# A two-layer hybrid decoder trunk with retrieved experts on one core: routing and gates head by head, the other heads beside a pair's own gathers

## The chip, the cores and the metric

One core of one Trainium2 chip runs the whole program in one launch. The time is device microseconds, from the start to the end of the execution. Engines are named as the profile names them: PE (TensorE), DVE (VectorE), ACT (ScalarE), POOL (GpSimd), SP (SyncE, which here only issues transfers).

## What is computed

512 tokens of width 1024 in float32 pass two layers. In each, a normalised input is projected and goes through three mixers (a Mamba-2 scan, stick-breaking attention, native sparse attention), whose outputs are projected and added to x. Then comes the expert layer:

```python
def block(xb):                                   # 128 tokens
    q = (xb @ w_q).reshape(Tb, PEER_HEADS, 2, half)            # 8 heads, two halves of 128
    s = jnp.einsum('thpd,pkd->thpk', q, sub_keys)              # 128 keys each
    sv, si = lax.top_k(s, PEER_TOPK)                           # 16
    cand = sv[:, :, 0, :, None] + sv[:, :, 1, None, :]
    cv, ci = lax.top_k(cand.reshape(Tb, PEER_HEADS, PEER_TOPK * PEER_TOPK), PEER_TOPK)
    i1 = jnp.take_along_axis(si[:, :, 0, :], ci // PEER_TOPK, axis=-1)
    i2 = jnp.take_along_axis(si[:, :, 1, :], ci % PEER_TOPK, axis=-1)
    eidx = i1 * N_KEYS + i2                                    # one of 16384 experts
    g = jax.nn.softmax(cv, axis=-1)
    u = u_tab[eidx]; v = v_tab[eidx]
    a = jax.nn.gelu(jnp.einsum('thkd,td->thk', u, xb))
    return jnp.einsum('thk,thkd->td', (g * a), v)
```

So each token reads 8 x 16 = 128 rows of 4 KB from each of two tables, its own rows.

## The kernel before

**Pairs, steps, slots.** The four blocks of 128 tokens go in pairs. A step is one pair of one layer; there are four (STEPS = 4). A step has a trunk (norm, mixers, output projection), a routing (queries, top 16, indices, gates), and 256 slots of gathers (PER_STEP): slot s reads one expert row for each of 128 tokens. POOL issues for each slot one indirect transfer of 512 KB from the u table (L1455) and, LAG = 20 slots later, one of 512 KB from the v table (L1468). Row buffers are rings of six (U_RING, V_RING): POOL may issue the u rows of slot s when the dot product of slot s - 6 is done.

**Who uses the rows.** DVE multiplies each u row by the normalised token and sums it (a dot, L1393). After 16 slots ACT takes the gelu and DVE multiplies by the gates (L1400). A v row is added to the output either by PE, as a product with a diagonal matrix of the weights (L741, two matmuls of 512 columns into `acc`, the diagonal made by ACT, L1021), or by DVE as one multiply-add (L1410). `of_vector` says which: before, DVE takes 1 of 2 while a trunk runs beside, 1 of 16 otherwise, and 1 of 4 in the last step. At a block's end `acc` is added to x (L1415).

**Order.** Each engine runs in the order of its program. The trunk and the routing are cut in phases (PHASES: n1a, ..., u0 to u24, cz, t0, ..., o0, ..., then the routing r0 to r22, each r from 4 on in three pieces r, rb, rc, and g0 to g2). SLOT_OF gives each phase a slot, and each engine, after its part of slot s, runs the phases due by s. Before, step 0's trunk and whole routing run first, with nothing gathered; then in the gathers of step n the trunk of step n + 1 stands in slots 22 to 146 and its routing in 146 to 253. The last step's gathers have nothing beside them.

**Routing.** Phase r k computes on PE the queries of half-head k (k = 0 to 15) and the scores of half-head k - 2; ACT copies both out of PSUM, the scores only when DVE is done with the half-head two before (`top`). DVE takes the top 16 of half-head k - 4 for both blocks, of the 256 sums of head (k - 6) // 2 for one block, and decodes the choice of k - 7 into table rows. After r22, g0 turns all eight heads' choices into indices at once (L1356, L1357: signal `idx`), ACT exponentiates all gates, g2 normalises them. POOL waits for `idx` once for each step; DVE waits for `gate` at each block's start (L1386).

Of the kernel before, what the change touches and what calls it, by code (L numbers as in the profile page):

```python
# [15 lines left out]
EXPERTS = KEYS * KEYS  # L17
# [134 lines left out]
def phases():  # L152
# [28 lines left out]
    tail += [("g0", 0, .4), ("g1", 0, 0), ("g2", 0, 1.2)]  # L181
# [17 lines left out]
SLOT_OF = slots()  # L199

# [4 lines left out]
           g_sub=1, g_exp=1, gate=1, idx=1, h2=2)  # L205


def trunk(nc, x_dram, const_dram, param_dram, w_dram, u_dram, v_dram, out_dram):
# [4 lines left out]
    with ctx:  # L213
# [163 lines left out]
        class Phases:  # L377


            def __init__(self, tracks):  # L380
                self.tracks = [[t, next(t)] for t in tracks]
                self.done = 0

            def upto(self, last):
                while self.done <= last:
                    for track in self.tracks:
                        while track[1] == PHASES[self.done][0]:
                            track[1] = next(track[0], None)
                    self.done += 1
                if last == len(PHASES) - 1:  # L390
                    assert all(at is None for _, at in self.tracks), self.tracks
# [22 lines left out]
        def phase_after(n, slot):  # L414

            return int((SLOT_OF <= slot - (n - 1) * PER_STEP).sum()) - 1

# [306 lines left out]
        def tensor_program(pe):  # L724
            run = Phases(tensor_tracks(pe, 0))
            run.upto(len(PHASES) - 1)
            for s in range(GATHERS + LAG):
                n = s // PER_STEP + 1
                if s % PER_STEP == 0 and n < STEPS:
                    run = Phases(tensor_tracks(pe, n))  # L730
# [13 lines left out]
                if n < STEPS:  # L744
                    run.upto(phase_after(n, s))


        def scalar_tracks(act, n, chain):
# [219 lines left out]
            def out_():  # L968
# [11 lines left out]
                for k in range(1, 2 * PEER_H + 3):  # L980
# [7 lines left out]
                    if k >= 3:  # L988
# [11 lines left out]
        def scalar_program(act):  # L1000
            chain = InOrder(act, "scalar_chain")
            run = Phases(scalar_tracks(act, 0, chain))
            run.upto(len(PHASES) - 1)
            for s in range(GATHERS + LAG):
                n = s // PER_STEP + 1
                if s % PER_STEP == 0 and n < STEPS:
                    run = Phases(scalar_tracks(act, n, chain))
# [14 lines left out]
                if n < STEPS:  # L1022
                    run.upto(phase_after(n, s))


        def vector_tracks(dve, n, chain):
# [295 lines left out]
            def route():  # L1322
# [46 lines left out]
        def vector_program(dve):  # L1369
# [3 lines left out]
            for s in range(GATHERS + LAG):  # L1373
# [42 lines left out]
                if n < STEPS:  # L1416
                    run.upto(phase_after(n, s))
# [125 lines left out]
```

## Time and profile before

| what | us |
|---|---|
| three runs: median (lowest, highest) | 3396.27 (3394.38, 3422.13) |
| the profiled execution, its own time | 3410.22 |
| its span on the profile page | 3408.4 |
| granted TensorE clock, mean | 0.924 |
| DVE, PE, POOL, ACT busy, share of the span | 69%, 78%, 66%, 23% |
| indirect transfers | 2048, 1073.9 MB |
| read from HBM over the span | 1183 MB, 348 GB/s |

The page cuts the span in 40 slices of 85.2 us; a digit is the busy share of a slice in tenths. The profiled execution's own time stands 14 us over the median, so a difference is worked out inside the profile and then taken from the median. A window of a view names its start and end from the span's start, and the x in it counts instructions; where a window is cut at POOL's issues of L1455, that count is its number of slots.

### The profile page before, as it was taken

To read this page: it belongs to the slowest core of one execution; us is meant where nothing else is said; L and a number is where in the kernel's file an instruction comes from. 1 tells how busy PE (TensorE), PEld (TensorE's weight loads), DVE (VectorE), ACT (ScalarE), POOL (GpSimd) and SP (SyncE) were. 2 spreads that over 40 slices of the span, in tenths; PEclk is the share of its full clock that TensorE was granted. 3 is DMA by queue.
4 is the path that set the end of the run, shared out by engine and by line. 5 is a ranking of instruction groups with operands and counts; after the bars stand their busy time and mean duration, and the time that the engine had idled before them with its cause. 6 is when DMAs were issued, how large, how long until landed. Compare 5 with 4: busy or idle time off the path is not lost.

```text
span 3408.4 us, 30404 instructions
## 1 busy us (share of the span) xinstructions
PE 2653.3 (78%) x9120; PEld 1550.1 (45%) x9120; DVE 2352.5 (69%) x5335; ACT 769.2 (23%) x1848; POOL 2260.1 (66%) x2059
## 2 busy tenths in 40 slices
PE   8888079898987689778987679988987666556657
PEld 7677057556543256446543246656543222112212
DVE  2327975877689576877699666877689755666564
ACT  2531023442211123332111122442211111111111
POOL 0000276777777776777777776777677777777776
PEclk9879589989999999878999999989999989998899
DMA  5112399999999999999999999999999999999999
GB/s 184 59 50 92 115 385 412 366 322 392 410 362 358 388 410 412 390 331 381 410 381 379 358 383 411 378 322 367 410 394 355 364 401 409 409 409 408 410 409 349
DMA packets 311313, 1187.53 MB, mean 348 GB/s; under 512 B 34544, under 2 KB 34544, under 8 KB 298352
## 3 DMA queue, kind: packets, MB, share of 16 engines
q0 software_dynamic: 294912, 1073.87, 81.8%
q1 hardware_dynamic: 16240, 111.72, 8.4%
q8 instruction: 75, 1.23, 0.1%
q14 instruction: 86, 0.70, 0.1%
HBM read 1183.36 MB, written 2.10 MB: 348 GB/s over the span
## 4 chain that ended last, share of the span: by engine, by line
POOL 30%; PE 26%; DMA 22%; issue 10%; DVE 4%; ACT 1%; ACTq 0%; DVEq 0%; POOLq 0%
DMA v_rows<-expert_v,idx 22%; POOL u_rows L1455 16%; POOL v_rows L1468 15%; PE acc L741 14%; PE bank L457 4%; PE bank L448 4%; DVE arena L1030 1%; PE bank L620 1%; PE bank L439 1%; DVE arena L1288 0%; PE bank L540 0%; DVE arena L1280 0%; DVE arena L1292 0%; DVE X L1410 0%; DVE arena L1318 0%
## 5 line engine op out<-in xcount | busy, mean ns | idle before, releaser
L741 PE MATMUL acc<-v_rows,diag 128*128 128x512 f32 x2988 | 1533.6, 647 | 647.4 <-DMA v_rows<-expert_v,idx 575.6
L1393 DVE CUSTOM_DVE_ANT_0 u_rows<-u_rows,h 128x1024 f32<-128x1024 f32 x1024 | 1247.9, 1224 | 650.5 <-DMA u_rows<-expert_u,idx 646.1
L1455 POOL DMA_INDIRECT u_rows<-expert_u,idx x1024 | 1122.4, 1096 | 685.4 <-DVE idx L1357 348.9
L1468 POOL DMA_INDIRECT v_rows<-expert_v,idx x1024 | 1133.9, 1107 | 404.3 <-issue 249.3
L741 PEld LDWEIGHTS acc<-v_rows,diag 128*128 128x128 f32 x2988 | 560.1, 203 | 1453.1 <-issue 1177.3
L1021 ACT ACTIVATE diag<-consts,wgt 128x128 f32<-128x128 f32 x747 | 286.2, 397 | 1097.8 <-PE acc L741 882.2
L448 PE MATMUL bank<-HT,w_ring 128*128 128x256 f32 x1792 | 405.1, 381 | 2.1 <-DVE HT L1030 2.1
L1410 DVE SCALAR_TENSOR_TENSOR X<-v_rows,wgt,X 128x1024 f32<-128x1024 f32 x277 | 355.7, 1284 | 56.4 <-DMA v_rows<-expert_v,idx 50.7
L448 PEld LDWEIGHTS bank<-HT,w_ring 128*128 128x128 f32 x1792 | 341.3, 191 | 81.3 <-issue 38.7
L457 PE MATMUL bank<-w_ring,HT 128*128 128x256 f32 (+1 forms) x1280 | 274.7, 372 | 0.0
L457 PEld LDWEIGHTS bank<-w_ring,HT 128*128 128x128 f32 x1280 | 236.7, 191 | 50.0 <-issue 21.4
L753 ACT ACTIVATE arena<-bank 128x256 f32<-128x256 f32 (+4 forms) x304 | 112.5, 382 | 505.4 <-PE bank L448 223.6
L1013 ACT ACTIVATE gel<-dots 128x16 f32<-128x16 f32 x64 | 13.8, 216 | 418.4 <-DVE dots L1393 418.3
L1030 DVE TENSOR_TENSOR arena<-arena 128x256 f32<-128x256 f32 (+3 forms) x238 | 102.4, 433 | 5.2 <-ACT arena L753 3.5
L1393 DVE DVE_READ_ACCUMULATOR2_ANT dots<- 128x1 f32 x1024 | 83.1, 81 | 0.0
L1280 DVE MAX8 arena<-arena 128x8 f32<-128x128 f32 (+1 forms) x192 | 52.8, 327 | 15.6 <-ACT arena L753 13.4
L620 PE MATMUL bank<-arena,w_ring 64*64 64x32 f32 x512 | 47.4, 267 | 20.1 <-issue 20.1
L670 PE MATMUL bank<-nkT,arena 64*128 64x128 f32 (+3 forms) x128 | 58.8, 545 | 3.5 <-ACT arena L949 3.5
L439 PE MATMUL bank<-dg,X 128*128 128x128 f32 x256 | 38.2, 318 | 28.9 <-ACT dg L753 28.9
L1288 DVE MATCH_REPLACE8 arena<-arena 128x128 f32<-128x128 f32 (+1 forms) x192 | 59.5, 318 | 0.0
L1030 DVE TENSOR_TENSOR HT<-bank,params 128x512 f32<-128x512 f32 x48 | 31.5, 685 | 40.3 <-PE bank L439 40.2
L1030 DVE TENSOR_TENSOR arena<-arena,consts 128x256 f32<-128x256 f32 (+3 forms) x168 | 58.6, 387 | 0.7
(185 smaller groups left out, 1860.1 us busy)
## 6 DMA issues: line engine op xcount, KB each, us to landing
w_ring<-weights SPq DMA_DIRECT2D x100, 1024.0 KB, 8.0
u_rows<-expert_u,idx POOLq DMA_INDIRECT x1024, 7.9
v_rows<-expert_v,idx POOLq DMA_INDIRECT x1024, 7.9
X<-in_x SPq DMA_DIRECT2D x2, 1024.0 KB, 6.5
out<-X SPq DMA_DIRECT2D x4, 512.0 KB, 6.5
n2w_wide<-parameters SPq DMA_DIRECT2D x2, 512.0 KB, 8.0
params<-parameters SPq DMA_DIRECT2D x2, 412.0 KB, 7.8
consts<-constants SPq DMA_DIRECT2D x1, 749.5 KB, 6.3
```

Of the source, the lines that this page charges most:

```text
L439: last = T.matmul(out[:, blk[i]], src[:, k * P:(k + 1) * P], dg[:, at_d + b], start=True, stop=True)
L448: last = T.matmul(out[:, 0:PAIR], cols(i)[:, k, m % 2 * P:(m % 2 + 1) * P], HT[:, k, :], start=(k == 0), stop=(k == KT - 1))
L457: last = T.matmul(out[:, 0:width], HT[:, k, blk[b]], cols(i)[:, k, 0:width], start=(k == 0), stop=(k == KT - 1))
L620: last = T.matmul(out[0:64, 0:CMP_PAD], weights[lo:lo + 64, j, :], cmp_z[lo:lo + 64, j, :], start=(j == 0), stop=(j == CMP_LEN - 1))
L741: last = T.matmul(acc[:, at_h], diag[:, i % DIAG_RING], v_rows[:, t % V_RING, at_h], start=(at_t == 0), stop=(t == max(q for q in range(t ...
L753: return S.activation(dst, src, ACT.Copy, **k)
L1021: made(S.activation(diag[:, i % DIAG_RING], ident, ACT.Copy, scale=wgt[:, b % 2, at_t:at_t + 1]), "diag")
L1030: return V.tensor_tensor(out, in0, in1, op)
L1393: made(V.tensor_tensor_reduce(out=rows_u, in0=rows_u, in1=h2[:], scale=1.0, scalar=0.0, op0=ALU.mult, op1=ALU.add, accum_out=dots[:, b % 2 ...
L1410: made(V.scalar_tensor_tensor(Xb, v_rows[:, t % V_RING, :], wgt[:, b % 2, at_t:at_t + 1], Xb, ALU.mult, ALU.add), "v_used_vector")
L1455: pool.indirect_dma_start(out=u_rows[:, s % U_RING, :], out_offset=None, in_=u_dram, in_offset=bass.IndirectOffsetOnAxis(ap=idx[:, (n - 1) ...
L1468: pool.indirect_dma_start(out=v_rows[:, t % V_RING, :], out_offset=None, in_=v_dram, in_offset=bass.IndirectOffsetOnAxis(ap=idx[:, t // PE ...
```

## The change

Routing and gates are made head by head. Indices of a head and block are formed as soon as they are decoded (`chosen`), a head's gates two phases later (`gated`), and POOL waits for the indices of the first block at every head. The phases before r8, which give head 0 of the first block, stay ahead of the pair's gathers; the rest, r8 to r22 and g2, stand beside the pair's own gathers in slots 1 to 86. The next trunk and its r0 to r7 follow in slots 90 to 254. DVE takes 1 of 2 v rows wherever the row's slot plus 20 is 90 or more (1 of 4 in the last step), 1 of 16 below that. The number of v rows that DVE adds goes from 71, 71, 71, 64 in the four steps to 97, 97, 97, 51.

```diff
@@
-TRUNK_AT, ROUTE_AT, DONE_AT = LAG + 2, 146, PER_STEP - 3
+
+ROUTED_AT, TRUNK_AT, FIRST_AT = 86, 90, PER_STEP - 2
 
 def of_vector(t):
     step, slot = divmod(t, PER_STEP)
-    if step == STEPS - 1:
-        return t % 4 == 3
-    return t % 2 == 1 if TRUNK_AT <= slot + LAG < ROUTE_AT else t % 16 == 15
+    if slot + LAG < TRUNK_AT:
+        return t % 16 == 15
+    return t % 4 == 3 if step == STEPS - 1 else t % 2 == 1
@@
-    tail += [("g0", 0, .4), ("g1", 0, 0), ("g2", 0, 1.2)]
+    tail += [("g2", 0, .5)]
@@
+FIRST = ORDER["r8"]
+
 def slots():
-    work = np.array([max(cost) + .5 for _, *cost in PHASES])
-    at, out = ORDER["r0"], []
-    for part, lo, hi in ((work[:at], TRUNK_AT, ROUTE_AT), (work[at:], ROUTE_AT, DONE_AT)):
-        out += list(lo + (np.cumsum(part) - part) / part.sum() * (hi - lo))
-    return np.array(out)
+    work = np.array([max(cost) + .5 for _, *cost in PHASES[:FIRST]] + [cost[1] + .5 for _, *cost in PHASES[FIRST:]])
+    spread = lambda part, lo, hi: lo + (np.cumsum(part) - part) / part.sum() * (hi - lo)
+    before_, beside = spread(work[:FIRST], TRUNK_AT - PER_STEP, FIRST_AT - PER_STEP), spread(work[FIRST:], 1, ROUTED_AT)
+    out = [n * PER_STEP + np.concatenate([before_ if n else np.full(FIRST, -1), beside]) for n in range(STEPS)]
+    return np.concatenate(out)
@@
+assert all(SLOT_OF[ORDER[f"r{7 + 2 * h}c"]] <= 16 * h - 5 for h in range(1, PEER_H))
@@ PER: how often each signal is given in a step
-           g_sub=1, g_exp=1, gate=1, idx=1, h2=2)
+           g_sub=8, g_exp=8, gate=8, idx=16, h2=2)
@@
-        def phase_after(n, slot):
-            return int((SLOT_OF <= slot - (n - 1) * PER_STEP).sum()) - 1
+        def phases_after(slot):
+            return int((SLOT_OF <= slot).sum())
@@ all four engine programs, as the tensor engine's
-            run = Phases(tensor_tracks(pe, 0))
-            run.upto(len(PHASES) - 1)
+            run = Phases(lambda n: tensor_tracks(pe, n))
+            run.upto(phases_after(-1))
             for s in range(GATHERS + LAG):
-                n = s // PER_STEP + 1
-                if s % PER_STEP == 0 and n < STEPS:
-                    run = Phases(tensor_tracks(pe, n))
...
-                if n < STEPS:
-                    run.upto(phase_after(n, s))
+                run.upto(phases_after(s))
@@ scalar_tracks, out_
-                yield "g1"
-                act.wait_ge(sig("g_sub"), nth(n, "g_sub", 1))
-                made(S.activation(g[:, n % 2], g[:, n % 2], ACT.Exp), "g_exp")
+                    if k >= 8 and k % 2 == 0:
+                        h = (k - 8) // 2
+                        at_h = g[:, n % 2].rearrange("p (b h k) -> p b h k", b=2, h=PEER_H)[:, :, h]
+                        act.wait_ge(sig("g_sub"), nth(n, "g_sub", h + 1))
+                        made(S.activation(at_h, at_h, ACT.Exp), "g_exp")
@@ vector_tracks, route
-                yield "g0"
-                g3 = g[:, n % 2].rearrange("p (b h k) -> p b h k", b=2, h=PEER_H)
+                        if b:
+                            made(tt(gates(h), cv[:, :, h], cv[:, :, h, 0:1].to_broadcast([P, 2, TOPK]), ALU.subtract), "g_sub")
+                    if 0 <= c - 1 < 2 * PEER_H:
+                        chosen(*divmod(c - 1, 2))
+                    if k >= 9 and k % 2:
+                        gated((k - 9) // 2)
+                yield "g2"
+                gated(PEER_H - 1)
+
+            def chosen(h, b):
                 chain.upto(chain.n)
-                made(tt(g3, cv, cv[:, :, :, 0:1].to_broadcast([P, 2, PEER_H, TOPK]), ALU.subtract), "g_sub")
-                chain(V.scalar_tensor_tensor(picked[:, 1], picked[:, 0], float(KEYS), picked[:, 1], ALU.mult, ALU.add))
-                made(V.tensor_scalar(idx[:, n % 2], picked[:, 1].rearrange("p b s -> p (b s)"), float(l * EXPERTS), None, ALU.add), "idx")
-                yield "g2"
-                dve.wait_ge(sig("g_exp"), nth(n, "g_exp", 1))
-                gsum = sm["gsum"][:].rearrange("p (b h) -> p b h", b=2)
-                chain(V.tensor_reduce(gsum, g3, AX.X, ALU.add))
-                chain(V.reciprocal(sm["grec"][:], sm["gsum"][:]))
-                made(tt(g3, g3, over(sm["grec"][:].rearrange("p (b h) -> p b h", b=2), TOPK)), "gate")
+                at_h = slice(h * TOPK, (h + 1) * TOPK)
+                chain(V.scalar_tensor_tensor(picked[:, 1, b, at_h], picked[:, 0, b, at_h], float(KEYS), picked[:, 1, b, at_h],
+                                             ALU.mult, ALU.add))
+                made(V.tensor_scalar(idx[:, n % 2, b * SLOTS + h * TOPK:b * SLOTS + (h + 1) * TOPK], picked[:, 1, b, at_h],
+                                     float(l * EXPERTS), None, ALU.add), "idx")
+
+            def gated(h):
+                dve.wait_ge(sig("g_exp"), nth(n, "g_exp", h + 1))
+                gsum, grec = (sm[name][:].rearrange("p (b h) -> p b h", b=2)[:, :, h] for name in ("gsum", "grec"))
+                chain(V.tensor_reduce(gsum, gates(h), AX.X, ALU.add))
+                chain(V.reciprocal(grec, gsum))
+                made(tt(gates(h), gates(h), over(grec, TOPK)), "gate")
@@ vector_program
                     if at_s == 0:
-                        m = n - 1
-                        dve.wait_ge(sig("rs5"), nth(m, "rs5", 1))
-                        dve.wait_ge(sig("gate"), nth(m, "gate", 1))
-                        dve.wait_ge(sig("n2w_in"), 16 * (m // PAIRS + 1))
+                        dve.wait_ge(sig("rs5"), nth(n, "rs5", 1))
+                        dve.wait_ge(sig("n2w_in"), 16 * (n // PAIRS + 1))
@@
                     dve.wait_ge(sig("gelu"), head + 1)
+                    dve.wait_ge(sig("gate"), nth(b // 2, "gate", head % PEER_H + 1 if b % 2 == 0 else PEER_H))
@@ pool_program
-                    if s % PER_STEP == 0:
-                        pool.wait_ge(sig("idx"), n)
+                    head = s % PER_STEP // TOPK
+                    if s % TOPK == 0 and head <= PEER_H:
+                        pool.wait_ge(sig("idx"), nth(n, "idx", 2 * head + 1 if head < PEER_H else 2 * PEER_H))
...
-                    run.upto(phase_after(n, s - POOL_LAG) if s % PER_STEP < PER_STEP - 1 else len(PHASES) - 1)
+                run.upto(phases_after(s - POOL_LAG))
```

Three places show what moves. On DVE at the start of the first gathers, after the first routing, before the change (g and idx are the gates and the indices, ISA is a dot and the read of its sum, h the normalised token):

```order
L1030 TENSOR_TENSOR g<-arena 128x256
L1356 SCALAR_TENSOR_TENSOR arena<-arena 128x256
L1357 TENSOR_SCALAR idx<-arena 128x256
L1361 TENSOR_REDUCE sm_gsum<-g 128x16
L1362 RECIPROCAL sm_grec<-sm_gsum 128x16
L1030 TENSOR_TENSOR g<-g,sm_grec 128x256
L1386 SCALAR_TENSOR_TENSOR h<-X,sm_rs,n2w_wide 128x1024
L1393 ISA u_rows,dots<-u_rows,h 128x1024
```

The same place after the change, which comes when only r0 to r7 have run:

```order
L1036 TENSOR_TENSOR g<-arena 128x2x16
L1375 SCALAR_TENSOR_TENSOR arena<-arena 128x16
L1377 TENSOR_SCALAR idx<-arena 128x16
L1405 SCALAR_TENSOR_TENSOR h<-X,sm_rs,n2w_wide 128x1024
L1412 ISA u_rows,dots<-u_rows,h 128x1024
L1412 ISA dots 128x1
L1412 ISA u_rows,dots<-u_rows,h 128x1024
L1412 ISA dots 128x1
L1036 TENSOR_TENSOR arena<-arena 128x256
L1286 MAX arena<-arena 128x8 x3
```

The indices cover 16 columns and not 256, and r8's top-16 work (the last two rows) now stands behind the first two dots.

On DVE after the change, across the boundary between steps 0 and 1 (the first rows are the end of r7's piece rc; L1430 is a v row added by DVE):

```order
L1036 TENSOR_TENSOR g<-arena 128x2x16
L1375 SCALAR_TENSOR_TENSOR arena<-arena 128x16
L1377 TENSOR_SCALAR idx<-arena 128x16
L1412 ISA u_rows,dots<-u_rows,h 128x1024
L1412 ISA dots 128x1
L1412 ISA u_rows,dots<-u_rows,h 128x1024
L1412 ISA dots 128x1
L1430 SCALAR_TENSOR_TENSOR X<-v_rows,wgt,X 128x1024
L1405 SCALAR_TENSOR_TENSOR h<-X,sm_rs,n2w_wide 128x1024
```

Two dots (slots 254 and 255) stand between the indices and the next step's normalised token (`h`); before, the indices came one slot earlier, ahead of the dots of 253 to 255.

On POOL at the first gathers after the change, with what each row waits for:

```order
L1473 DMA u_rows<-expert_u,idx 128x1024 [waits idx,tail]
L1473 DMA u_rows<-expert_u,idx 128x1024 x5
L1473 DMA u_rows<-expert_u,idx 128x1024 [waits u_used] x10
L1473 DMA u_rows<-expert_u,idx 128x1024 [waits u_used,idx]
L1473 DMA u_rows<-expert_u,idx 128x1024 [waits u_used] x4
L1486 DMA v_rows<-expert_v,idx 128x1024
```

A second wait for `idx` stands at slot 16 and again at every 16th slot up to 128: nine in a step, where there was one.

## Rows read from the trace of the kernel before

**Rows 1.** The page: busy shares, then tenths busy in 40 slices, and GB/s.

```profile
PE 2653.3 (78%) x9120; PEld 1550.1 (45%) x9120; DVE 2352.5 (69%) x5335; ACT 769.2 (23%) x1848; POOL 2260.1 (66%) x2059
...
POOL 0000276777777776777777776777677777777776
...
GB/s 184 59 50 92 115 385 412 366 322 392 410 362 358 388 410 412 390 331 381 410 381 379 358 383 411 378 322 367 410 394 355 364 401 409 409 409 408 410 409 349
```

**Rows 2.** The u transfers (L1455) alone, by step; the last step in three.

```profile
core 0: us, POOL busy (x), PEclk, DMA share, GB/s
397.85:1148.22 750.37, 293.88 (x256) 0.94 0.98 374
1148.22:1924.55 776.33, 291.27 (x256) 0.93 0.99 385
1924.55:2701.85 777.30, 285.97 (x256) 0.95 0.99 376
2701.85:2927.00 225.15, 83.11 (x86) 0.92 1.02 402
2927.00:3363.00 436.00, 167.72 (x170) 0.94 1.03 409
```

**Rows 3.** All engines by stretch: routing alone, first gathers, step 1's trunk, its routing, two 16-slot stretches.

```profile
core 0: us, PE busy (x) PEld busy (x) DVE busy (x) ACT busy (x) POOL busy (x), PEclk, DMA share, GB/s
275.00:296.00 21.00, 21.00 (x109) 18.75 (x108) 17.89 (x99) 3.44 (x11) 0.00 (x0) 1.00 0.35 121
296.00:397.00 101.00, 35.11 (x158) 29.07 (x156) 99.01 (x466) 6.78 (x20) 0.00 (x0) 0.70 0.13 48
397.85:425.00 27.15, 0.00 (x0) 0.00 (x0) 20.02 (x33) 0.22 (x1) 21.31 (x20) 0.50 0.91 325
...
1209.70:1592.80 383.10, 324.24 (x1297) 214.00 (x1296) 287.20 (x475) 118.12 (x277) 285.26 (x251) 0.90 0.99 382
1592.80:1924.55 331.75, 270.95 (x794) 141.95 (x793) 268.75 (x814) 60.23 (x158) 256.46 (x220) 0.97 1.00 385
1828.40:1877.10 48.70, 36.70 (x76) 14.13 (x74) 48.15 (x169) 7.42 (x21) 38.95 (x33) 0.91 0.98 370
3117.50:3158.40 40.90, 28.29 (x48) 11.03 (x48) 24.82 (x38) 4.81 (x13) 31.18 (x32) 0.83 1.03 409
```

**Rows 4.** POOL's waits in step 1's trunk stretch, 1209.70 to 1592.80: total, times, longest.

```profile
POOL u_rows L1455 <- issue: 36.5, 120, 0.3
POOL v_rows L1468 <- issue: 32.3, 106, 0.3
POOL v_rows L1468 <- PE acc L741: 23.5, 18, 4.3
POOL u_rows L1455 <- DVE dots L1393: 5.5, 4, 2.4
```

**Rows 5.** The page's groups: dots, their reads, DVE's v rows.

```profile
L1393 DVE CUSTOM_DVE_ANT_0 u_rows<-u_rows,h 128x1024 f32<-128x1024 f32 x1024 | 1247.9, 1224 | 650.5 <-DMA u_rows<-expert_u,idx 646.1
...
L1410 DVE SCALAR_TENSOR_TENSOR X<-v_rows,wgt,X 128x1024 f32<-128x1024 f32 x277 | 355.7, 1284 | 56.4 <-DMA v_rows<-expert_v,idx 50.7
...
L1393 DVE DVE_READ_ACCUMULATOR2_ANT dots<- 128x1 f32 x1024 | 83.1, 81 | 0.0
```

**Rows 6.** DVE in order of time: the first rows of r7 and of r8; then idx.

```profile
288.53 0.43 DVE L1030 TENSOR_TENSOR arena<-arena 128x256 f32<-128x256 f32 x1
...
295.86 0.43 DVE L1030 TENSOR_TENSOR arena<-arena 128x256 f32<-128x256 f32 x1
...
396.69 0.29 DVE L1357 TENSOR_SCALAR idx<-arena 128x256 uint32<-128x256 f32 x1
```

**Rows 7.** POOL in order of time: the first gather.

```profile
397.90 1.14 POOL L1455 DMA_INDIRECT u_rows<-expert_u,idx  x1 [348.88 <-DVE idx L1357]
```

**Rows 8.** DVE in order of time, end of step 0's gathers: idx.

```profile
1145.27 0.29 DVE L1357 TENSOR_SCALAR idx<-arena 128x256 uint32<-128x256 f32 x1
```

**Rows 9.** POOL in order of time: step 1's first u transfer.

```profile
1148.27 0.93 POOL L1455 DMA_INDIRECT u_rows<-expert_u,idx  x1 [0.30 <-issue]
```

More of the change, by code:

```diff
@@ L377, in trunk, with __init__, upto @@
         class Phases:
[L380 to L385, printed above, removed]
+            def __init__(self, tracks_of):
+                self.tracks_of, self.done = tracks_of, 0
+            def upto(self, count):
+                while self.done < count:
+                    n, i = divmod(self.done, len(PHASES))
+                    if i == 0:
+                        self.tracks = [[t, next(t)] for t in self.tracks_of(n)]
                     for track in self.tracks:
-                        while track[1] == PHASES[self.done][0]:
+                        while track[1] == PHASES[i][0]:
                             track[1] = next(track[0], None)
                     self.done += 1
-                if last == len(PHASES) - 1:
-                    assert all(at is None for _, at in self.tracks), self.tracks
+                    if i == len(PHASES) - 1:
+                        assert all(at is None for _, at in self.tracks), self.tracks
         def over(scalars, n):
@@ L979, in out_ @@
                     diagonal("5", b, 0)
-                for k in range(1, 2 * PEER_H + 3):
+                for k in range(1, 2 * PEER_H + 7):
                     yield f"r{k}"
@@ L1001, in scalar_program @@
             chain = InOrder(act, "scalar_chain")
-            run = Phases(scalar_tracks(act, 0, chain))
-            run.upto(len(PHASES) - 1)
+            run = Phases(lambda n: scalar_tracks(act, n, chain))
+            run.upto(phases_after(-1))
             for s in range(GATHERS + LAG):
-                n = s // PER_STEP + 1
-                if s % PER_STEP == 0 and n < STEPS:
-                    run = Phases(scalar_tracks(act, n, chain))
                 if s % TOPK == 0 and 0 < s <= GATHERS:
@@ L1021, in scalar_program @@
                     made(S.activation(diag[:, i % DIAG_RING], ident, ACT.Copy, scale=wgt[:, b % 2, at_t:at_t + 1]), "diag")
-                if n < STEPS:
-                    run.upto(phase_after(n, s))
+                run.upto(phases_after(s))
         def vector_tracks(dve, n, chain):
@@ L1370, in vector_program @@
             chain = InOrder(dve, "vector_chain")
-            run = Phases(vector_tracks(dve, 0, chain))
-            run.upto(len(PHASES) - 1)
+            run = Phases(lambda n: vector_tracks(dve, n, chain))
+            run.upto(phases_after(-1))
             for s in range(GATHERS + LAG):
-                n = s // PER_STEP + 1
-                if s % PER_STEP == 0 and n < STEPS:
-                    run = Phases(vector_tracks(dve, n, chain))
+                n = s // PER_STEP
                 if s < GATHERS:
@@ L1415, in vector_program @@
                     made(V.tensor_tensor(Xb, acc[:], Xb, ALU.add), "x_done")
-                if n < STEPS:
-                    run.upto(phase_after(n, s))
+                run.upto(phases_after(s))
         def pool_tracks(pool, n, chain):
@@ L1442, in pool_program @@
             chain = InOrder(pool, "pool_chain")
-            run = Phases(pool_tracks(pool, 0, chain))
-            run.upto(len(PHASES) - 1)
+            run = Phases(lambda n: pool_tracks(pool, n, chain))
+            run.upto(phases_after(-1))
             for s in range(GATHERS + LAG):
-                n = s // PER_STEP + 1
-                if s % PER_STEP == 0 and n < STEPS:
-                    run = Phases(pool_tracks(pool, n, chain))
+                n = s // PER_STEP
                 if s < GATHERS:
-                    if s % PER_STEP == 0:
-                        pool.wait_ge(sig("idx"), n)
+                    head = s % PER_STEP // TOPK
+                    if s % TOPK == 0 and head <= PEER_H:
+                        pool.wait_ge(sig("idx"), nth(n, "idx", 2 * head + 1 if head < PEER_H else 2 * PEER_H))
                     if s >= U_RING:
```

8 lines of the change are left out of this document (5 added, 3 removed).

## Prediction

> **What bounds the kernel now.** I began with the page. No engine is busy all through, and for the first four and a half of 40 slices POOL does nothing while from then on the bytes come at 320 to 412 GB/s [rows 1]. So the program has two parts: a start without gathers, and a stretch in which something paces them. The time line of POOL dates the border: its first transfer starts at 397.90, 348.88 us late, released by `idx` [rows 7].
>
> The second part is 3010.5 us, and the windows of the u transfers cut it by steps [rows 2]: 750.4, 776.3, 777.3, then 225.2 for the first 86 slots of the last step, 436.0 for the other 170, and 3408.4 - 3363.0 = 45.4 behind them. A slot costs 2.93, 3.03, 3.04, 2.62 and 2.56 us. I read what paces it from three rows [rows 3]:
> - With nothing beside (3117.50 to 3158.40, 16 slots, 2.56 a slot) POOL is busy 31.18 us in 32 transfers, 0.97 each, and rests 0.30 before each: 2 x (0.97 + 0.30) = 2.55. POOL's own issuing is the pace; DVE is busy 61%.
> - Beside the densest routing (1828.40 to 1877.10, 16 slots, 3.04 a slot) the transfers take 38.95 / 33 = 1.18 and the rest is the same: 2 x 1.48 = 2.96. DVE is busy 99%. POOL waits for nobody, each issue is longer.
> - Beside the trunk (1209.70 to 1592.80, 124 slots, 3.09 a slot) a transfer takes 285.3 / 251 = 1.14. POOL idled for PE 23.5 us in 18 times, for DVE 5.5 in 4 [rows 4]; less the 0.3 that stands before any transfer that is 22 us. Without them the pace is (383.1 - 22) / 124 = 2.91.
>
> So outside the start the kernel is at POOL's issue rate, 2.56 us a slot when DVE is loosely used and about 2.9 to 3.0 when it is dense, plus waits where PE is late.
>
> **The start.** Before, r8 to r22 stand between the end of r7 and the indices. r8's first row starts at 295.86, the indices at 396.69 [rows 6], POOL 1.21 behind them [rows 7]. After, r7 ends with three small rows (gates' subtraction, two for the indices), 0.6 us by the gaps of the rows around them, so indices are made at 296.5 and the first transfer starts at 297.7. That is **-100.2 us**. Nothing hides it and nothing is uncertain in it but tenths; all that can be lost is what the moved work costs further on: 99.0 us of DVE and 35.1 of PE [rows 3].
>
> **DVE's load of a slot.** A dot is 1224 + 81 ns, so 1.30; a v row on DVE 1284 ns [rows 5]: 0.64 a slot where it takes 1 of 2, 0.08 at 1 of 16. A full routing phase is 295.86 - 288.53 = 7.3 us [rows 6]. The trace has no per-head gates and indices. Eight small rows a head replace six wide ones; between 0.1 (all pipelined) and 0.3 us each (the indices' row took 0.29) gives 0.8 to 2.4 us a head; less 0.3 for the removed share I take 1.3, 0.65 a phase, 10 us in a step. With 5.65 slots between phases (85 slots, 15 phases) the routing is (7.3 + 0.65) / 5.65 = 1.41 a slot.
>
> **Slots 0 to 20 of steps 1 to 3.** The v rows of the previous step's end are still half DVE's: 1.30 + 0.64 + 1.41 + 0.1 for normalising and closing a block (two rows of 1024 columns, like those of [rows 5], in 20 slots) = 3.45. That is over POOL's 2.96, so here DVE would be the pace. POOL runs two to five dots ahead and the ring allows six, so up to 10 us of it could be absorbed (low end 2.96 a slot); I charge it in full: 69 us.
> **Slots 0 to 20 of step 0.** No v rows. DVE needs 2.8 a slot; POOL issues slot 20 when dot 14 is done: 5 us to the first landing + 14 x 2.8 = 44 us, against 28 before (20 transfers in 27.15 us, as DVE keeps up with the dots alone) [rows 3].
> **Slots 20 to 86.** DVE 1.30 + 0.08 + 1.41 = 2.8, a little under the dense row's 3.0. Pace 2.95 (bounds: 2.75, half way between the loose and the dense row; 3.10, the dense row's 3.04 with the added small rows on top): 66 x 2.95 = 195.
> **Slots 86 to 90.** Nothing beside: 10 us.
> **The trunk, n1a to n2a, slots 90 to 233.** The same work on 143 slots instead of 124, so the parts on PE are 13% less dense. No-wait pace 2.90 as now, 415 us; PE's waits, 22 us now, I halve to 12 (bounds 0 and 22): 427. PE's load falls on the whole (DVE takes 26 v rows more in a step, each two matmuls fewer for PE).
> **r0 to r7, slots 233 to 256.** DVE's part (275 to 296) is 17.9 us [rows 3], plus 1.3, in the last 17 slots: 1.13 + 1.94 = 3.07 and lumps of up to 3 us. I charge 3.15 x 23 = 73.
> **The boundary.** Before, the indices were made at 1145.27 [rows 8] and POOL needed them at 1148.27 [rows 9], 3 us to spare. After, they follow dot 253, one slot later, and 3.1 us of r7's last piece: at about 1150.5, and later when DVE is behind, as it is there. Queued behind POOL's wait are the v transfers of slots 236 on. I charge 5 us at each of three boundaries (bounds 0, if POOL is held up anyway, and 12, with DVE three rows behind).
>
> The nine waits for `idx` in a step cost nothing by the order: head 1 is due after slot 10 and asked for at 16, the others have more. The cover is six dots, 17 us; without it each would cost its lateness. The new wait for `gate` is met seven slots ahead.
>
> **The sum**, in the profile's own time:
>
> | step | before | after | difference |
> |---|---|---|---|
> | start | 397.9 | 297.7 | -100.2 |
> | 0 | 750.4 | 44 + 195 + 10 + 427 + 73 = 749 | -1 |
> | 1 | 776.3 | 5 + 69 + 195 + 10 + 427 + 73 = 779 | +3 |
> | 2 | 777.3 | 779 | +2 |
> | 3, to slot 86 | 225.2 | 5 + 69 + 195 = 269 | +44 |
> | rest | 481.4 | the same | 0 |
>
> Together -52: 3410.2 becomes 3358. The median stands 14 lower, so the forecast is **3344 us**.
>
> **A page's rule against the rows.** In the stretch with nothing beside, DVE is 61% busy with dots and v rows alone, and POOL's transfers take 0.97; beside routing they take 1.18 with the same number of dots [rows 3].
> The Trainium skill, page "SBUF — State Buffer", section "Who interferes with whom", says that a DVE instruction with two SBUF inputs contends with a GpSimd instruction that reads SBUF, and one with at most one does not (outside the two-port modes). Dots and v rows have two such inputs; top-16 rows have one. By it alone slots 20 to 86 would stay near 2.6 a slot, 23 us a step less than I charge. The row on routing disagrees, so the sum goes by the row; no run here separates the forms of instruction.
>
> **Rivals.**
> - *Forecast (0.50).* As summed; its own range 3318 to 3370.
> - *The cover is cheaper (0.17).* Routing spread over 85 slots leaves DVE at 2.8 a slot, and issues lengthen only where DVE is really full. Then slots 20 to 86 go at 2.75 (-13 in each of four steps) and the overload of slots 0 to 20 is absorbed by the ring (-10 in three): 3344 - 82 = 3262 at the most; half of that is likelier, 3303. For it: POOL at 1.14 beside the trunk, where DVE is 75% busy; against it: beside the routing of step 1 DVE is busy 81% and a transfer takes 256.5 / 220 = 1.17 already.
> - *DVE becomes the bound (0.22).* From slot 239 of a step to 20 of the next, 37 slots, DVE's need is over POOL's pace. If its in-order waits (for ACT's copies, for v rows that are late) add 0.15 us a slot there and in slots 20 to 86, that is 3 x 37 + 4 x 66 = 375 slots x 0.15 = 56 us. The gain is gone: 3400. For it: 99% busy in the dense stretch; against: POOL did not wait for DVE even there.
> - *Indices come late, head by head (0.11).* POOL's wait at a head holds the v transfers behind it too, and PE and DVE behind those. There are 28 new heads; from 52 / 28 = 1.9 us of lateness each the gain is gone, and at 5 us each, two slots, the kernel takes 3344 + 140 = 3484; at 3.5 us it takes 3442. For it: DVE will run late in slots 0 to 20, where head 1 has only six slots of cover; against: heads 2 to 7 gain 4.7 slots of cover each.
>
> **How the numbers follow.** About 1%, 34 us, is what a measurement of this kernel can tell from no change: faster is under 3362, slower over 3430. The forecast lies under 3362 in nine tenths of its weight: 0.45 + 0.17 = 0.62 faster; the rest of the forecast, the third case and a little of the last are within 1%: 0.28; slower 0.10, nearly all from late indices. The range must leave out no more than 0.2. Below it goes to the second case, 3303, rounded to 3300 (both cheap ends in full, 3262, are the tail that is left out); above it takes in the third case, 3400.
>
> **What would show it.** POOL's first u transfer at 297.7. In the windows by step, 749, 779, 779, and 269 for the first 86 slots of the last, then again 2.56 a slot. POOL's mean transfer near 1.17 in slots 20 to 86 of the last step, where it was 0.98. DVE over 95% busy in slots 240 to 276. POOL waiting for `idx` at three boundaries for some 5 us and at the heads not at all; its waits for PE in the trunk stretch halved. The prediction is wrong if POOL waits for dots or indices by tens of microseconds, or if a step's 256 slots take under 765 or over 795.

## The result, and the profile after

| | before | after |
|---|---|---|
| median of 20 runs each, us | 3410.88 | 3389.13 |
| lowest, highest | 3393.79, 3434.49 | 3373.11, 3405.5 |
| the profiled execution | 3410.22 | 3384.28 |
| its span | 3408.4 | 3382.5 |

The ratio is 0.9931, 95% interval [0.9912, 0.9950]: 22 us, or 0.7%, where 52 us, 1.5%, had been forecast. That is faster, but less than half as much as I said, and by my own bound of 1% it is no change. The profiled executions, in whose time the sum was made, differ by 25.9 us. (The median of three runs shown ahead of the prediction, 3396.27, was 15 us low. The sum does not hang on it, the 3344 does: from the 20 runs it would have been 3359.)

The page of after, the lines that answer to [rows 1]:

```profile
PE 2623.9 (78%) x8860; PEld 1549.2 (46%) x8860; DVE 2455.5 (73%) x5632; ACT 810.0 (24%) x1860; POOL 2313.6 (68%) x2059
...
POOL 0002777767776787767775777767777678777776
...
GB/s 183 62 41 193 360 368 375 412 410 354 347 399 355 365 340 389 411 411 368 348 390 365 387 369 359 388 411 343 356 370 411 351 358 337 363 408 408 409 409 360
```

POOL starts a good slice earlier, and the stretch at 408 to 410 GB/s at the end is shorter, with 337 to 363 ahead of it. The u transfers of after by step, as in [rows 2]:

```profile
core 0: us, POOL busy (x), PEclk, DMA share, GB/s
297.75:1061.73 763.98, 289.97 (x256) 0.91 0.98 373
1061.73:1849.00 787.27, 287.85 (x256) 0.90 0.98 376
1849.00:2639.00 790.00, 286.13 (x256) 0.91 0.98 374
2639.00:2899.05 260.05, 104.54 (x86) 0.91 0.95 350
```

The first transfer starts at 297.78, where 297.7 was forecast. A window here runs up to the next step's first transfer, so the boundary's 5 us belong to the step before it: forecast were 754, 779 and 779, and 264 for the last step's first 86 slots. The steps take 764, 787 and 790 us, the 86 slots 260.

All engines of after, by stretches (slots 20 to 86, 90 to 233 and 233 to 256 of step 0; then slots 0 to 20 and 20 to 86 of the last step):

```profile
core 0: us, PE busy (x) PEld busy (x) DVE busy (x) ACT busy (x) POOL busy (x), PEclk, DMA share, GB/s
340.10:533.45 193.35, 136.61 (x328) 58.52 (x328) 174.21 (x570) 41.83 (x99) 152.19 (x132) 0.95 0.98 366
544.00:977.50 433.50, 381.04 (x1565) 249.74 (x1564) 325.62 (x526) 142.41 (x309) 330.88 (x287) 0.93 0.99 380
977.50:1061.73 84.23, 67.15 (x254) 46.30 (x252) 67.26 (x171) 14.99 (x36) 53.03 (x46) 0.91 0.97 390
...
2639.00:2698.40 59.40, 34.93 (x96) 19.72 (x96) 53.74 (x148) 8.27 (x21) 46.49 (x40) 0.80 0.94 356
2698.40:2899.05 200.65, 144.43 (x352) 65.20 (x352) 174.51 (x564) 41.66 (x98) 159.73 (x132) 0.94 0.95 348
```

The third row is the one that stands out: 23 slots in 84.2 us, 3.66 a slot. What POOL did there, in order of time:

```profile
1045.71 1.14 POOL L1473 DMA_INDIRECT u_rows<-expert_u,idx  x1 [0.30 <-issue]
1047.16 0.95 POOL L1486 DMA_INDIRECT v_rows<-expert_v,idx  x1 [0.30 <-issue]
1061.75 1.67 POOL L1473 DMA_INDIRECT u_rows<-expert_u,idx  x1 [13.65 <-DVE idx L1377]
```

and DVE, up to the indices that POOL waits for (the first two rows are the dot of slot 253 and a v row, the rest the end of r7):

```profile
1056.38 1.22 DVE L1412 CUSTOM_DVE_ANT_0 u_rows<-u_rows,h 128x1024 f32<-128x1024 f32 x1
...
1057.52 1.28 DVE L1430 SCALAR_TENSOR_TENSOR X<-v_rows,wgt,X 128x1024 f32<-128x1024 f32 x1
...
1059.65 0.72 DVE L1324 TENSOR_REDUCE arena<-arena 128x16 f32<-128x256 f32 x2
...
1061.31 0.17 DVE L1377 TENSOR_SCALAR idx<-arena 128x16 uint32<-128x16 f32 x1
```

POOL issued slot 255 at 1045.71, as early as the ring of six allows: dot 249 was done, dot 250 in hand. Ahead of the indices DVE still had the rest of that dot, dots 251 to 253, two v rows and the last pieces of r6 and r7, and it did them with hardly a gap, busy 15.19 of 15.60 us (columns as above, from POOL's issue to the row of `idx`):

```profile
1045.71:1061.31 15.60, 9.08 (x30) 4.92 (x28) 15.19 (x58) 0.96 (x3) 2.09 (x2) 0.84 0.77 312
```

POOL stood still 13.65 us; at the two later boundaries 14.90 and 13.65. Before, the indices had been 3 us early.

### The profile page after: what moved, and what is told of

The parts are those of the page before. It is cut to its first block, busy times and chain, and to the rows that moved or that the text cites. A ratio compares the mean times of both kernels' runs of the same rounds, so it can differ in the third digit from the quotient of the medians.

```text
span 3382.5 us, 30188 instructions
## 1 busy us (share of the span) xinstructions
PE 2623.9 (78%) x8860; PEld 1549.2 (46%) x8860; DVE 2455.5 (73%) x5632; ACT 810.0 (24%) x1860; POOL 2313.6 (68%) x2059
## 4 chain that ended last, share of the span: by engine, by line
POOL 33%; PE 22%; DMA 20%; issue 11%; DVE 6%; ACT 1%; DVEq 0%; ACTq 0%; POOLq 0%
DMA v_rows<-expert_v,idx 18%; POOL v_rows L1486 17%; POOL u_rows L1473 16%; PE acc L750 13%; PE bank L469 3%; PE bank L460 3%; DMA u_rows<-expert_u,idx 2%; DVE u_rows L1412 2%; PE bank L632 1%; DVE X L1430 1%; PE bank L451 1%; DVE arena L1036 1%; DVE arena L1286 0%; DVE arena L1294 0%; DVE arena L1298 0%
## 5 line engine op out<-in xcount | busy, mean ns | idle before, releaser
L750 PE MATMUL acc<-v_rows,diag 128*128 128x512 f32 x2728 | 1489.1, 683 | 672.6 <-DMA v_rows<-expert_v,idx 598.3
L1473 POOL DMA_INDIRECT u_rows<-expert_u,idx x1024 | 1134.1, 1108 | 625.0 <-issue 303.2
L1486 POOL DMA_INDIRECT v_rows<-expert_v,idx x1024 | 1177.0, 1149 | 385.6 <-issue 259.4
L750 PEld LDWEIGHTS acc<-v_rows,diag 128*128 128x128 f32 x2728 | 534.4, 212 | 1417.0 <-issue 1181.4
L1430 DVE SCALAR_TENSOR_TENSOR X<-v_rows,wgt,X 128x1024 f32<-128x1024 f32 x342 | 439.7, 1286 | 73.6 <-DMA v_rows<-expert_v,idx 67.1
L1028 ACT ACTIVATE diag<-consts,wgt 128x128 f32<-128x128 f32 x682 | 256.1, 395 | 850.8 <-PE acc L750 644.2
L460 PE MATMUL bank<-HT,w_ring 128*128 128x256 f32 x1792 | 412.9, 386 | 3.2 <-DVE HT L1036 3.2
L460 PEld LDWEIGHTS bank<-HT,w_ring 128*128 128x128 f32 x1792 | 350.0, 196 | 97.7 <-issue 53.4
L957 ACT ACTIVATE arena<-bank,sm_nm 128x128 f32<-128x128 f32 (+3 forms) x64 | 33.7, 526 | 120.8 <-DVE sm_nm L1235 57.7
L451 PE MATMUL bank<-dg,X 128*128 128x128 f32 x256 | 40.3, 329 | 25.9 <-ACT dg L761 25.9
```

Source lines behind the costliest of these rows:

```text
L451: last = T.matmul(out[:, blk[i]], src[:, k * P:(k + 1) * P], dg[:, at_d + b], start=True, stop=True)
L460: last = T.matmul(out[:, 0:PAIR], cols(i)[:, k, m % 2 * P:(m % 2 + 1) * P], HT[:, k, :], start=(k == 0), stop=(k == KT - 1))
L750: last = T.matmul(acc[:, at_h], diag[:, i % DIAG_RING], v_rows[:, t % V_RING, at_h], start=(at_t == 0), stop=(t == max(q for q in range(t ...
L1028: made(S.activation(diag[:, i % DIAG_RING], ident, ACT.Copy, scale=wgt[:, b % 2, at_t:at_t + 1]), "diag")
L1430: made(V.scalar_tensor_tensor(Xb, v_rows[:, t % V_RING, :], wgt[:, b % 2, at_t:at_t + 1], Xb, ALU.mult, ALU.add), "v_used_vector")
L1473: pool.indirect_dma_start(out=u_rows[:, s % U_RING, :], out_offset=None, in_=u_dram, in_offset=bass.IndirectOffsetOnAxis(ap=idx[:, n % 2, ...
```

## The experiments

All figures are ratios to the kernel before, run beside each on the same chip; after is 0.9931. The runs stand in three groups, each on a chip of its own: x_first248, x_v16, x_both and x_route0_first; x_both240, x_last16 and x_quarter; x_first251 and x_first240. A difference of two ratios times 3411 is given in us. An interval is some 0.004 to either side, 13 us, so two of these runs are told apart only if they differ by some 18 to 20 us, and a run and after (0.002 to either side) by some 15.

| run | ratio, interval | against after |
|---|---|---|
| x_first251 | 0.9874 [0.9831, 0.9916] | -19 |
| x_first248 | 0.9821 [0.9783, 0.9859] | -38 |
| x_first240 | 0.9891 [0.9854, 0.9927] | -14 |
| x_v16 | 0.9854 [0.9815, 0.9893] | -26 |
| x_both | 0.9749 [0.9703, 0.9794] | -62 |
| x_both240 | 0.9811 [0.9778, 0.9844] | -41 |
| x_quarter | 0.9796 [0.9764, 0.9828] | -46 |
| x_last16 | 0.9767 [0.9733, 0.9801] | -56 |
| x_route0_first | 1.0117 [1.0059, 1.0174] | +63 |

### The first indices earlier

```diff
-ROUTED_AT, TRUNK_AT, FIRST_AT = 86, 90, PER_STEP - 2
+ROUTED_AT, TRUNK_AT, FIRST_AT = 86, 90, 248
```

> The changed kernel with one number changed: the trunk and r0 to r7 of the next pair are spread over slots 90 to 248 instead of 90 to 254, so that the first indices of the next pair follow dot 247 and not dot 253. Theory (late indices): in the changed kernel POOL waits 13.6 us for the indices at each of three boundaries, because DVE is full over slots 240 to 254 and five dots behind; six slots of lead are about 17 us, so the wait falls below 2 us at each boundary and the kernel gets 30 to 40 us shorter than the changed one (some 3350 to 3360 where that has 3389). Rival (zero sum): DVE has the same rows to do by slot 20 of the next step, so the time comes back as waits for dots or as a slower pace in slots 0 to 20, and the kernel stays within 10 us of the changed one.

It measured 38 us less than after, near the theory's upper end. No boundary wait for indices is left, and slots 233 to 256 take 72.6, 74.3 and 71.7 us where after has 84.2, 86.5 and 83.9. Slots 0 to 20 of the next step take 58.2, 58.3 and 61.2 (59.1, 58.9 and 59.4 in after): the time did not come back there. The zero-sum rival is out. A dose between, 251:

> The changed kernel with the trunk and r0 to r7 of the next pair spread to slot 251 (254 in the changed kernel, 248 in an earlier run). A dose: POOL's wait at a boundary was 13.6 to 14.9 us at 254 and 1 or less at 248. If the wait is the indices' place in DVE's order and nothing else, three slots earlier take about 3 x 3 us off: a wait of 4 to 6 us at each boundary and a total half way between the two (about 0.988 of the kernel before). If the wait comes from something that is merely late at that moment (a v row, a copy of ACT), it stays at 10 or more.

POOL at the first boundary of that run, in order of time:

```profile
1057.21 0.94 POOL L1486 DMA_INDIRECT v_rows<-expert_v,idx  x1 [0.30 <-issue]
1062.45 1.66 POOL L1473 DMA_INDIRECT u_rows<-expert_u,idx  x1 [4.30 <-DVE idx L1377]
```

4.30 us for 13.65 (4.33 at the two later boundaries), and 0.9874, half way between. So 254, 251 and 248 give 13.7, 4.3 and nothing: the wait is set by the indices' place in DVE's order, three slots being some 9 us. The total alone does not tell 251 from 248, 18 us apart; the waits do.

### DVE's v rows around the boundary

```diff
     if slot + LAG < TRUNK_AT:
         return t % 16 == 15
+    if slot + LAG >= 236 and step < STEPS - 1:
+        return t % 16 == 15
     return t % 4 == 3 if step == STEPS - 1 else t % 2 == 1
```

> The changed kernel, but DVE adds only 1 of 16 v rows (not 1 of 2) where the row stands in slots 236 to 276 of a step (the last 20 and the next step's first 20). PE adds them instead. Theory (DVE full at the end of a step): about 8 rows of 1.28 us leave DVE ahead of the indices, so POOL's wait at each boundary falls from 13.6 us to about 3, and DVE is no longer full in slots 0 to 20; 25 to 35 us less than the changed kernel. Rival (PE is needed there): PE gets 17 rows of 1.3 us more at each boundary, beside r0 to r7, is late with its v rows, and holds POOL; the gain is under 10 us or turns into a loss.

26 us less. POOL at the first boundary:

```profile
1057.50 0.94 POOL L1488 DMA_INDIRECT v_rows<-expert_v,idx  x1 [0.30 <-issue]
1066.75 1.66 POOL L1475 DMA_INDIRECT u_rows<-expert_u,idx  x1 [8.31 <-DVE idx L1379]
```

The wait fell by 5.3 us and not by 10 (to 9.49 and 8.31 at the later boundaries): eight v rows, 10 us, left DVE ahead of the indices, but only two of them had stood behind POOL's issue of slot 255, where POOL waits. The other 10 us of the gain lie outside this wait. PE took the rows without being late: POOL's waits for it come to 113.7 us in this run and 123.3 in after. The theory holds in direction, its size was too large; the rival is out.

> Both edits of the two runs before together: the first indices due at slot 248, and 1 of 16 v rows for DVE over slots 236 to 276. Theory (late indices are the whole loss): it ends within 5 us of the better of the two alone, since either one takes the wait away. If DVE's load mattered beyond the wait, it is 10 us or more better than the better of the two.

The second outcome: 0.9749 is 25 us better than the better of the two alone, so the v rows on DVE cost something beyond the wait. The windows of slots 0 to 20 and 20 to 86 of its last step:

```profile
core 0: us, PE busy (x) PEld busy (x) DVE busy (x) ACT busy (x) POOL busy (x), PEclk, DMA share, GB/s
2588.40:2643.10 54.70, 44.88 (x121) 22.33 (x122) 45.28 (x143) 11.35 (x28) 42.50 (x40) 0.94 1.02 407
2643.10:2837.55 194.45, 147.55 (x377) 66.43 (x375) 174.68 (x564) 42.32 (x100) 152.97 (x132) 0.98 0.98 366
```

With DVE busy 45.3 us and not 53.7 in the 20 slots, a transfer takes 42.50 / 40 = 1.06 against 46.49 / 40 = 1.16 in after, and the stretch 54.7 against 59.4 (in steps 1 and 2 it is 1.09 and 1.12 against 1.15 twice). In the other 66 slots DVE's rows are the same in all kernels; the 1.16 against 1.21 there is no effect of the edit, for x_first248 has 1.16 too. Shorter waits and issues account for about 18 us over the three boundaries (slots 0 to 20: 10, slots 233 to 256: 8, against x_first248); the rest is within what two profiles differ by. This kernel has the lowest ratio of all I ran, and is clearly faster than the kernels before and after.

### How dense the trunk stands

> The changed kernel with the trunk and r0 to r7 of the next pair spread to slot 240, eight slots before the run with 248 (0.982), DVE's v rows unchanged. It asks whether a denser trunk costs. The prediction's term: PE's waits in the trunk stretch fall in proportion to how thin the trunk is spread. By that, 150 slots instead of 158 cost some 4 us a step, 10 to 15 in all: 0.986. If density does not matter between these spreads, it is the time of 248 within 5 us.

0.9891, 24 us more than with 248: the direction of the prediction's term, and about twice its size. POOL's waits in slots 90 to 233 of step 2, first in after, then in this run:

```profile
POOL v_rows L1486 <- PE acc L750: 25.6, 18, 4.3
POOL u_rows L1473 <- DVE dots L1412: 5.2, 4, 1.9
```

```profile
POOL v_rows L1486 <- PE acc L750: 37.2, 18, 5.5
POOL u_rows L1473 <- DVE dots L1412: 8.3, 5, 4.6
```

Eighteen times each, but longer. Less the 0.3 before any transfer, all waits in slots 90 to 233 of steps 0, 1 and 2 are 16, 21 and 25 us in after, 19, 36 and 32 with 251, 27, 27 and 29 with 248, 39, 30 and 39 with 240. How far two kernels differ by chance shows in x_both and x_last16, which are alike in these three steps: 77 us and 95.

> The changed kernel with the trunk and r0 to r7 spread over slots 90 to 240 (not 254) and 1 of 16 v rows for DVE from slot 228 of a step to 20 of the next. It goes a step further in the direction of the run with both edits (248 and 236), which measured 0.975 of the kernel before. Theory (the boundary wait is gone at 248 already; what is left is POOL's own issuing): no more gain; denser trunk phases add PE waits, so 0 to 15 us more than the run with both edits. Rival (DVE's fullness still costs at the boundary): 5 to 15 us less.

0.9811, 21 us more than both edits at 248. The theory's direction again, over its upper end. In the profiles slots 233 to 256 of the three steps get 17 us shorter, since part of r0 to r7 has left them, and slots 90 to 233 get 23 us longer.

```diff
+    if slot + LAG >= 236 and step < STEPS - 1:
+        return t % 16 == 15
-    return t % 4 == 3 if step == STEPS - 1 else t % 2 == 1
+    return t % 4 == 3
```

> The run with both edits, but beside the trunk DVE adds 1 of 4 v rows and not 1 of 2 (PE gets 146/4 = 37 rows of 1.3 us more in each of three steps). Theory (PE is what is late beside the trunk): POOL's waits for PE in slots 90 to 233 double at least and the kernel gets 30 us or more longer than with both edits. Rival (DVE's load is what lengthens POOL's issues there, 1.14 us against 0.98): transfers get shorter by some 0.05 us and the kernel gains up to 30 us.

16 us more than both edits at 248, which the intervals do not tell apart; the profiles show what moved. POOL's waits for PE in slots 90 to 233 of step 0, first with both edits, then here:

```profile
POOL v_rows L1488 <- PE acc L752: 30.2, 17, 4.3
```

```profile
POOL v_rows L1488 <- PE acc L752: 48.1, 30, 6.0
```

Both theories are right in part: the waits grow by 11 to 19 us in each step (they do not double), and the transfers get 0.02 us shorter, 0.012 to 0.027 by step, some 6 us in 286 of them. PE weighs more: slots 90 to 233 of the three steps together take 25 us longer. So one half for DVE looks the better share beside the trunk; the totals do not prove it.

### What lengthens POOL's issues

> The run with both edits, and DVE adds 1 of 16 v rows (not 1 of 4) in the whole last step too. It asks how POOL's issues depend on DVE's rows where nothing stands beside: in slots 96 to 256 of the last step a slot takes 2.56 us with transfers of 0.98 us. If rows of two SBUF inputs lengthen an issue, fewer of them (0.24 us less DVE work a slot) shorten it towards the 0.94 of an undisturbed one: 2.50 a slot, some 8 us less in 160 slots. If the pace is set by something else, it stays at 2.56 and the time is that of both edits, within 5 us.

The edit on top of both is `step == STEPS - 1` joined to the condition for 1 of 16. Slots 96 to 233 of the last step, 137 slots:

```profile
2881.20:3235.80 354.60, 255.36 (x508) 89.74 (x507) 182.54 (x292) 49.84 (x136) 271.06 (x274) 0.97 1.02 405
```

and with both edits alone:

```profile
2865.00:3220.70 355.70, 236.57 (x409) 88.08 (x408) 214.14 (x317) 40.60 (x111) 271.83 (x276) 0.86 1.02 405
```

DVE is busy 182.5 and not 214.1 us; a transfer takes 0.989 against 0.985. 25 fewer rows with two operands in SBUF change nothing here, and the ratio, 0.9767, is that of both edits within its interval.

That does not clear those rows, as single issues show. From the last step of after, slots 20 to 86, six of POOL's issues:

```profile
2722.08 1.45 POOL L1486 DMA_INDIRECT v_rows<-expert_v,idx  x1 [0.30 <-issue]
2723.84 1.19 POOL L1473 DMA_INDIRECT u_rows<-expert_u,idx  x1 [0.30 <-issue]
...
2726.83 1.74 POOL L1473 DMA_INDIRECT u_rows<-expert_u,idx  x1 [0.30 <-issue]
2728.88 0.94 POOL L1486 DMA_INDIRECT v_rows<-expert_v,idx  x1 [0.30 <-issue]
...
2731.37 1.80 POOL L1486 DMA_INDIRECT v_rows<-expert_v,idx  x1 [0.30 <-issue]
2733.47 0.94 POOL L1473 DMA_INDIRECT u_rows<-expert_u,idx  x1 [0.30 <-issue]
```

and what DVE had in hand when each of them began:

```profile
2721.50 1.22 DVE L1412 CUSTOM_DVE_ANT_0 u_rows<-u_rows,h 128x1024 f32<-128x1024 f32 x1
...
2723.79 0.42 DVE L1036 TENSOR_TENSOR arena<-arena 128x256 f32<-128x256 f32 x1
...
2726.56 1.21 DVE L1412 CUSTOM_DVE_ANT_0 u_rows<-u_rows,h 128x1024 f32<-128x1024 f32 x1
...
2728.83 0.09 DVE L1294 MATCH_VALUE_LOAD arena<-arena 128x8 f32 x1
2728.91 0.28 DVE L1294 MATCH_REPLACE8 arena<-arena 128x128 f32<-128x128 f32 x1
...
2731.13 1.22 DVE L1412 CUSTOM_DVE_ANT_0 u_rows<-u_rows,h 128x1024 f32<-128x1024 f32 x1
...
2733.21 0.72 DVE L1324 TENSOR_REDUCE arena<-arena 128x16 f32<-128x256 f32 x2
```

DVE is busy nearly all the time, yet two issues take 0.94: those that began beside rows with one input. The other four began inside a row with two inputs in SBUF, and each ended 0.8 us after that row: the dot from 2721.50 ends at 2722.72, the issue at 2723.53.

It is so in the whole trace of after. Of its 2048 issues 447 began with DVE idle and 82 with nothing but a top-16 row, a reduction or the read of a dot's sum in hand: all took 0.93 to 0.95. 814 began at least 0.1 us into a dot or v row that had 0.15 us or more to go: 811 of them ended 0.80 to 0.83 after that row, and they took 1.33 on average. The other ten traces show the same: of 8677 such issues in all eleven, 8656 ended in that span.

So an issue is lengthened by the one row that it falls upon, and a stretch by how its issues fall. Where nothing stands beside the gathers, DVE waits for its rows, and a dot that is in hand when an issue begins is nearly over: 0.2 us from its end, on average, in the last step of after. Beside the routing of that step it is 0.56 us from its end. That fits the 25 rows that did not matter: 9 issues and not 34 began in a v row, but 134 and not 131 in a dot. All issues of slots 20 to 86 of the last step together are 36 us over 0.94 each in after and 6 us before the change, and the stretch takes 200.6 us and not 170.1.

### What the early start is worth

```diff
-    out = [... np.concatenate([before_ if n else np.full(FIRST, -1), beside]) for n in range(STEPS)]
+    out = [... np.concatenate([before_ if n else np.full(FIRST, -1), beside if n else np.full(len(beside), -1)]) for n in range(STEPS)]
```

> The changed kernel, but the whole routing of the first pair runs ahead of its gathers, as before the change. It measures what the early start is worth net. Theory of the prediction: first gather about 107 us later (100 us and the small rows per head), step 0's first 86 slots about 40 us shorter, since nothing stands beside them (28 us for the first 20, 2.6 a slot for the other 66): 65 to 70 us longer than the changed kernel. Rival: POOL's issues in those slots are as long as before and the early start is worth its full 100 us.

63 us more than after (69 in the profiles), as expected, though not in the way expected. POOL's first six transfers go out as early as in after, since the first head's indices are there; then it stands:

```profile
409.27 1.68 POOL L1473 DMA_INDIRECT u_rows<-expert_u,idx  x1 [104.00 <-DVE dots L1412]
```

Slots 0 to 20 take 135.8 us, where after takes 42.3, and slots 20 to 86 take 176.0, where after takes 193.4. In the profiles the moved routing gives 93.5 us at the start and takes 17.4 back in the 66 slots. That the total fits is partly luck: 23 us had been expected back in the 66 slots and 16 in the first 20. The rival, the full 100 us, is out by the interval.

## Why the prediction was wrong

Its range held the time; its size did not: -52 forecast, -25.9 in the same pair of profiles. By its own terms, in us:

| term | forecast | measured | miss |
|---|---|---|---|
| start | 297.7 | 297.8 | 0 |
| slots 0 to 20, step 0 | 44 | 42.3 | -2 |
| slots 0 to 20, steps 1 to 3 | 69 each | 59.1, 58.9, 59.4 | -30 |
| slots 20 to 86, four steps | 195 each | 193.4, 194.6, 196.6, 200.6 | +5 |
| slots 86 to 90, steps 0 to 2 | 10 each | 10.6, 11.8, 11.0 | +3 |
| slots 90 to 233, steps 0 to 2 | 427 each | 433.4, 435.4, 439.6 | +27 |
| slots 233 to 256 and boundary | 73 + 5 each | 84.2, 86.5, 83.9 | +21 |
| rest of the last step | 481.4 | 483.4 | +2 |

They add up to +26. Three terms were wrong, two too low (the boundary and the trunk stretch) and one too high (slots 0 to 20 of steps 1 to 3), and that the total is still inside the range is luck: +27 and +21 against -30. By its own signs the prediction was wrong too: POOL waited 42 us for indices at the boundaries, and step 0 took under 765.

**The start** was right to a tenth, and so were slots 0 to 86 of the first step: 239 forecast, 235.7 measured.

**The boundary** is the step whose mechanism failed. I saw that the indices come one slot later and DVE would be behind, and charged 5 us with 12 as the upper bound. It was 13.7, 14.9 and 13.7. I had worked out DVE's need as 3.07 us a slot with lumps and set its backlog at one slot, at most three. In the rows the ring is full from slot 246 on: POOL has six u rows issued that are not yet used, and the dots of slots 250 to 254 come 3.0, 5.1, 3.4 and 5.0 us apart, with the pieces of r6 and r7 between them, as DVE's order demands. A wait on DVE's result does not begin at POOL's margin but at the end of this backlog, some 15 us. The runs with 251 and 248 show that the place of the indices sets the wait, x_v16 that DVE's load there does too. (Slots 233 to 256 without the wait, 70.6, 71.6 and 70.2, were well priced at 73.)

**Slots 0 to 20** failed to the other side. I charged DVE's full need, 3.45 a slot, and named the ring's absorption as the low end. DVE was busy 53.7 of 59.4 us, 2.7 a slot, and the pace was POOL's own, 2.95: transfers of 1.15 to 1.16 us, waits of under 1 us in all. DVE did 18 dots and 9 v rows in that time, which leaves about 1 us a slot to the routing where I had 1.41, and the ring took up the rest: three rows were issued and not yet used at slot 0, five at slot 20. It was not the stand at the boundary that made room for this: with 248 POOL does not stand, five rows are open at slot 0, and the stretch takes 58 to 61 us with waits of 0.9. I had charged the overload where it was free and nearly nothing where it had to be paid.

**The trunk stretch** was mis-sized, and it is the largest of the terms that were too low. I took the waits, nearly all for PE, to halve from 22 us (step 1's) to 12 when the trunk is spread 15% wider. They were 16, 21 and 25 (of 27, 22 and 29 before, by the same count), and the transfers stayed at 1.14 to 1.16. The granted clock hardly differed: 0.93, 0.90 and 0.92 in these stretches, 0.94, 0.90 and 0.95 before. Spreading does help: all three steps together wait 62 us at 254, 87 at 251, 83 at 248 and 108 at 240, two kernels alike there differing by up to 18; halving had no row behind it.

**The signs.** DVE was busy 86% of slots 240 to 276 and not over 95%, and a transfer in slots 20 to 86 of the last step took 1.21 where 1.17 had been forecast.

**The rivals.** Late indices were a rival of mine, but at the heads inside a step. These waits are 5.48 us once, at head 1 of the first step, and 1.0 at head 1 of the others; the mechanism was right and its place was the boundary. That DVE becomes the bound did not happen: POOL's waits for dots are 22.4 us in all, 31.7 before. The cheaper cover did not come either: slots 20 to 86 were priced right, at 2.95.

**The page's rule.** By the Trainium skill, "SBUF — State Buffer", section "Who interferes with whom", only DVE rows with two SBUF inputs contend with a POOL instruction that reads SBUF, outside the two-port modes. These traces agree: an issue, which reads its indices from SBUF, took 0.93 to 0.95 us beside top-16 rows and reductions and ended 0.8 us after a dot or v row that it fell upon. What failed is what I made of the rule, that slots 20 to 86 would stay near 2.6 because each slot has the same dots as in a loose stretch. They took 2.93 to 3.04, with transfers of 1.15 to 1.21 us. The number of dots is the same, but beside routing an issue falls upon them earlier, and some of the routing's own rows (TENSOR_TENSOR, 128x256) have two inputs too. In the sum this did no harm, since its pace came from the row. That it is the place of the dots and not the busy share is read from the rows of eleven traces; I ran nothing that moves the dots alone.

## What to carry to other kernels

When work is moved between stages of a software pipeline, look at what the moved work's consumer asks for first, and count the producer's backlog at that point, not its average load: a short overload is free as long as a ring absorbs it, and is paid in full, up to the ring's depth, at the first wait that needs the producer to be up to date. Put that hand-over a few slots ahead of its need. Six slots here were worth more than the whole change, 38 us against 22.

And when an instruction gets longer beside a busy engine, compare single instances before you blame the busy share: which row was in hand when it began. The mean of a stretch hid here that half the issues were not lengthened at all.

## What was not expected of the hardware

An indirect transfer's issue on POOL, which moves nothing itself, takes 0.94 us when DVE is idle or at a row with one input, however busy DVE is. If it begins 0.1 us or more into a dot or a v row, it ends 0.81 us after that row, so it takes up to 2.0 us (a few in all traces took 2.9 to 4.3). A row that adds PSUM to SBUF (`X<-acc,X`) lengthened none of the 77 issues that began beside it in the eleven traces: 0.95 us at most. Over 0.94 each, the 2048 issues cost 393 us in after and 338 us before the change, and 347 to 388 in the others. POOL's issues are the pace of this kernel, and its waits for PE and for dots together are 146 us in after. No run here tried to avoid the overlap.
